# Start of a two-block transformer forward on one core: the transpose of the first norm weights as a step of its own, warm-up transposes 14 + 24 made 16 + 18, and new step orders

## What is computed

```python
# first block: layer 0 (differential attention), layer 1 (causal attention)
z = rmsnorm(x, a_norm_attn) @ a_w_in                      # q, k, v, memory queries
kv = rmsnorm(mem, a_mem_norm) @ a_w_mem_kv                # memory keys and values
x = x + concat(diff_attention(q, k, v), memory_attention(qm, mem)) @ a_w_out
x = x + square(relu(rmsnorm(x) @ a_w_up)) @ a_w_down      # hidden 4096
...                                                       # layer 1: kv, b_w_in, memory, MLP
x = rmsnorm(x, final_norm)
# second block
qa, c, iq, ik, iw, qb, kb, vb, gb = split(rmsnorm(x) @ w_in_2)
out_a = indexed_sparse_attention(qa, c, iq, ik, iw, rel_bias_2)   # top 64 keys
out_b = silu(gb) * group_norm(retention(qb, kb, vb))
x = x + concat(out_a, out_b) @ w_out_2
x = x + (silu(h @ w_gate_2) * (h @ w_up_2)) @ w_down_2    # hidden 2816
```

## Time and profile before

| | |
|---|---|
| median of 3 runs | 928.08 us (926.46 to 929.03) |
| the profiled execution | 928.42 us |
| its span, first to last instruction | 926.7 us |
| outside the span | 1.7 us |
| PE busy | 917.0 us (99%) |
| DVE busy | 574.1 us (62%) |
| ACT busy | 473.4 us (51%) |

### The profile page before, as it was taken

One profiled execution on the slowest core, in us unless ns is written; L12 is line 12 of the kernel. 1 busy time (PEld: TensorE's weight loads), 2 busy tenths in 40 slices (PEclk: granted clock), 3 DMA queues, 4 the chain that ended last, 5 costly groups with the idle time before them and its releaser, 6 DMA issues.

```text
span 926.7 us, 13209 instructions
## 1 busy us (share of the span) xinstructions
PE 917.0 (99%) x4740; PEld 768.6 (83%) x4740; DVE 574.1 (62%) x779; ACT 473.4 (51%) x718; POOL 55.2 (6%) x126
## 2 busy tenths in 40 slices
PE   8999999999999999999999999999999999999998
PEld 7778788888888888788888888888887888888886
DVE  4768658655555668365855655677886555444453
ACT  5866557444444566654644444556456463444441
POOL 1202121000000000000200000002130010000000
PEclk9999999999999999999999999999999999999999
DMA  8945135655556534234755555455613255556541
GB/s 290 334 137 165 65 137 196 222 196 201 184 182 191 171 137 136 92 113 147 262 188 198 199 186 183 152 174 179 197 63 128 92 181 182 181 183 197 189 155 46
DMA packets 95435, 157.77 MB, mean 170 GB/s; under 512 B 5928, under 2 KB 37624, under 8 KB 95392
## 3 DMA queue, kind: packets, MB, share of 16 engines
q1 hardware_dynamic: 93824, 155.08, 50.1%
q10 hardware_dynamic: 1536, 2.11, 0.7%
q0 software_dynamic: 32, 0.02, 0.0%
HBM read 156.12 MB, written 1.06 MB: 170 GB/s over the span
## 4 chain that ended last, share of the span: by engine, by line
PE 96%; DVE 2%; issue 1%; ACT 1%; DMA 0%; ACTq 0%; POOL 0%
PE proj L1563 10%; PE proj L1565 10%; PE proj L1564 10%; PE score L1563 6%; PE score L1564 6%; PE score L1565 6%; PE outp L1565 6%; PE outp L1563 6%; PE outp L1564 6%; PE turn L1622 6%; PE proj L1622 6%; PE turn L1626 3%; PE proj L1626 3%; PE turn L1609 2%; PE outp L1812 2%; PE score L1774 2%
## 5 line engine op out<-in xcount | busy, mean ns | idle before, releaser
L1904 DVE TENSOR_TENSOR wlo<-raw,whi 128x2048 fp32r<-128x2048 f32 (+1 forms) x131 | 297.7, 2277 | 192.5 <-ACT whi L1331 147.6
L1331 ACT ACTIVATE whi<-raw 128x2048 fp32r<-128x2048 f32 x64 | 122.6, 1916 | 170.0 <-PE outp L1565 57.5
L1563 PE MATMUL proj<-whi,set 128*128 128x512 f32 (+1 forms) x428 | 169.5, 396 | 1.0 <-DVE set L2069 1.0
L1565 PE MATMUL proj<-whi,set 128*128 128x512 f32 (+1 forms) x428 | 165.7, 387 | 0.0
L1564 PE MATMUL proj<-wlo,set 128*128 128x512 f32 (+1 forms) x428 | 165.2, 386 | 0.0
L1320 ACT ACTIVATE whi<-raw 128x2048 fp32r<-128x2048 f32 (+1 forms) x67 | 126.7, 1897 | 51.4 <-PE outp L1565 17.2
L1563 PEld LDWEIGHTS proj<-whi,set 128*128 128x128 f32 x428 | 80.4, 188 | 17.9 <-issue 1.7
L1565 PEld LDWEIGHTS proj<-whi,set 128*128 128x128 f32 x428 | 80.3, 188 | 16.8
L1564 PEld LDWEIGHTS proj<-wlo,set 128*128 128x128 f32 x428 | 80.5, 188 | 14.9
L1563 PE MATMUL score<-whi,set 128*128 128x512 f32 x236 | 92.9, 393 | 0.0
L1563 PE MATMUL outp<-whi,set 128*128 128x512 f32 x236 | 92.4, 391 | 0.0
(11 more groups left out here) (228 smaller groups left out, 1171.9 us busy)
## 6 DMA issues: line engine op xcount, KB each, us to landing
raw<-in_a_w_up SPq DMA_DIRECT2D x32, 512.0 KB, 4.2
raw<-in_a_w_down SPq DMA_DIRECT2D x32, 512.0 KB, 4.2
raw<-in_b_w_up SPq DMA_DIRECT2D x32, 512.0 KB, 4.2
raw<-in_b_w_down SPq DMA_DIRECT2D x32, 512.0 KB, 4.6
raw<-in_w_gate SPq DMA_DIRECT2D x22, 512.0 KB, 4.0
raw<-in_w_up SPq DMA_DIRECT2D x22, 512.0 KB, 5.0
raw<-in_w_down SPq DMA_DIRECT2D x22, 512.0 KB, 4.1
raw<-in_a_w_in SPq DMA_DIRECT2D x20, 512.0 KB, 7.1
```

The source lines that it names most:

```text
L1331: act.activation(shaped(whi, u), shaped(raw, u), ACT.Copy).then_inc(hi_done, 1)
L1563: pe.matmul(out_, hi, wh, start=start, stop=False)
L1565: return pe.matmul(out_, lo, wh, start=False, stop=stop)
L1904: return dve.tensor_tensor(shaped(wlo, u)[:, ks, :], shaped(raw, u)[:, ks, :], shaped(whi, u)[:, ks, :], ALU.subtract)
```

## The change

1. A new step `first_gains` stands in the list behind `turn_operand 0` and `1`. PE's part of it is `turn_gains(0)` and then `warm_up(WARM[1])`; DVE's part is the copy to `gcol`. `setup` keeps PE's wait and `warm_up(WARM[0])`.
2. `WARM` is (16, 18) where it was (14, 24). The warm-up behind `turn_operand 1` is gone.
3. `MOVES` is new for all three engines. Its last pair for PE is `("first_gains 0", "turn_operand 0")`, and its last two for DVE are `("turn_operand 1", "turn_operand 0")` and `("first_gains 0", "turn_operand 1")`. Run through the list, they give PE: `setup`, `first_gains`, `turn_operand 0`, `turn_operand 1`, `multiply 0`; and DVE: `first_gains`, `turn_operand 1`, `turn_operand 0`, `split 0`. ACT's first eight steps are as before, save that `square_sum 0` now stands ahead of `turn_operand 4`.
4. DVE waits for `ka_done` ahead of `retention_out 0`.

```diff
@@ MOVES, "PE" (last entries)
-        ("multiply 9", "turn_heads 3"), ("turn_operand 7", "multiply 3"), ("turn_operand 6", "turn_operand 7"),
-        ("multiply 2", "turn_operand 6"),
+        ("turn_operand 7", "multiply 3"), ("turn_operand 6", "turn_operand 7"), ("multiply 2", "turn_operand 6"),
+        ("first_gains 0", "turn_operand 0"),
@@ MOVES, "DVE" (last entries)
-        ("turn_operand 7", "split 4"), ("turn_operand 6", "split 3"), ("split 2", "turn_operand 6"),
+        ("turn_operand 6", "split 4"), ("turn_operand 7", "turn_operand 6"), ("split 2", "split 3"),
+        ("turn_operand 1", "turn_operand 0"), ("first_gains 0", "turn_operand 1"),
...
-WARM = (14, 24)
+WARM = (16, 18)
@@ the list of steps
         m1 = [turn_mem(0)]
+        add("first_gains")
         split(1)
@@ PE
                 if st.kind == "setup":
                     pe.wait_ge(consts_made, 1)
                     warm_up(WARM[0])
+                elif st.kind == "first_gains":
                     turn_gains(0)
+                    warm_up(WARM[1])
...
                     turn_bank(n, lambda t, k: st.src[:, t, k * P:(k + 1) * P], [k0, k0 + 1])
-                    if st.name == "turn_operand 1":
-                        warm_up(WARM[1])
@@ DVE
-                if st.kind == "setup":
+                if st.kind == "first_gains":
                     dve.wait_ge(s_full, 1)
...
                 elif st.kind == "retention_out":
                     dve.wait_ge(o_full, st.o + 1)
+                    if st.p == 0:
+                        dve.wait_ge(ka_done, NT)
```

## The result

The changed kernel takes 932.23 us in the median of four runs (932.10 to 934.07), the kernel before 928.08 (926.46 to 929.03): 4.15 us more, ratio 1.0059 (1.0046 to 1.0072). The profiled execution is the slowest of the four, 934.07 us with a span of 932.3. The forecast was 928.7 with a range to 932.2 and slower at 0.24.

A forecast was written before the change was run, and what follows sets the result against it. PE was taken to bound the kernel, busy 917.0 of 926.7 us. The start's +1.4 and the later orders' -0.8 gave +0.6 on the median of 928.08: 928.7 us, with a range of 926.0 to 932.2.

The forecast's parts named there:

- The order at the start: PE's start: norm weights still first, 18 warm-ups ahead of the mem transposes, `multiply 0` at 13.7 for 12.35, +1.4 us.
- the term for the granted clock behind the gap: First products behind PE's new 2 us gap from 11.7: no cost for a low clock in the sum.
- rival A: PE's gap at the start: level rises late or falls, first products run at 1.2 GHz; +3.7, 931.8 us; chance 0.17.
- The prediction's own sign of being wrong: First products at the start: matmuls of 0.43 us following PE's gap would show the forecast wrong.
- the -0.8 for the orders: Later orders: PE's 1.0 and 0.7 us waits around the group norm could go; half taken, -0.8 us.
- DVE's wait for `ka_done`: Ahead of `retention_out 0`: waits for DVE's own step some 15 steps earlier, holds nothing behind it; cost 0.
- the two more warm-ups at first: First warm-up on PE, 16 for 14: ends at 5.3, covered by the wait for the norm weights; cost 0.
- DVE's bank 1 ahead of bank 0: Operand copies at the start: DVE starts only when ACT has done both banks at 12.35, ending at 13.65.
- Rival C: First warm-ups: 16 lift PE's clock before 6.4, `multiply 0` at 11.6; -1.5, 926.5 us; chance 0.10.
- Rival D: PE's start: mem transposed ahead of the norm weights as the title says, `multiply 0` at 10.7; 925.6 us; chance 0.05.

The follow-up runs named there:

- the start alone: Kernel before with only the changed start (first_gains and 18 warm-ups ahead of the mem transposes, 16 first, DVE bank 1 first), all other orders as before: 931.61 us.
- the orders alone: Kernel before with the changed kernel's later orders and its wait for `ka_done`, keeping its own start (14 and 24 warm-ups): 928.83 us.
- the twelve: Kernel before with 12 warm-ups behind the mem transposes in place of 24: 926.87 us.
- the table load behind: Changed kernel with one ACT pair left out, so turn_weights 33 stands ahead of exps 34 again: 930.22 us.
- Memory first: Kernel before with the changed start, but PE transposes mem first, then the norm weights, then 18 warm-ups, DVE's order to suit: 925.62 us.
- gap filled: Changed kernel with 18 more warm-ups behind turn_operand 1, in PE's gap ahead of the first multiply: 930.38 us.
- memory first with the new orders: Changed kernel with only its first entries mended (PE takes mem, then first_gains; DVE first_gains, bank 0, bank 1), later orders kept: 929.00 us.
- memory first with twelve: Kernel before with mem transposed ahead of the norm weights and 12 warm-ups behind these in place of 18 (`WARM = (16, 12)`): 925.55 us.
- no warm-ups: Kernel before with no warm-ups behind the mem transposes in place of 24 (`WARM = (14, 0)`): 928.68 us.

## Why the forecast was wrong

**The order at the start** was read rightly. PE still waited for the norm weights, the 18 warm-ups stood between them and `mem`, and the first product came at 13.79 where the forecast had 13.7. The gap was 2.1 us for 2. In the changed kernel's own profile that closeness is partly luck: the transposes began at 10.01, not 10.8, since the first of the 18 ran at the full level, and took 1.70 us, not 0.88, since the level had fallen. In the start alone the terms themselves came out: the 18 end at 10.67 and the first product starts at 13.85.

**The step that failed at the start is the term for the granted clock behind the gap, which the likeliest sum put at nothing.** The forecast left 0.17 to rival A, a level that is low behind that gap. It came in five runs of six (the start alone), and its price was 1.9 (931.6 for 929.72), for 2.1 in rival A. The argument against it was that no row showed a fall. But no row of before showed PE resting for 2 us soon after a rise either, so that was no evidence. The prediction's own sign of being wrong, matmuls of 0.43 us behind the gap, came. The rule of the Trainium skill, "TensorE: Matmul & The Clock Gate", Part 1, was weighed as something for single runs. The traces agree that the level comes down around rests and that the moment differs from run to run: the 18 warm-ups ahead of `mem` take 2.11 to 4.03 us in the profiles of the changed start. For the chance it was read too weakly.

Rival A's 931.8 lies near the measured 932.23, but its sum isn't what happened either. It had 4.5 us for the start, where 3.7 came, and -0.8 for the orders, which cost time.

**The step that failed behind it is the -0.8 for the orders.** Its sign was wrong. The forecast followed DVE's queue and PE's, and both came out: the waits of 1.0 and 0.7 around the group norm went. It didn't follow ACT's, where `exps 34` now stood between two copies of weights, with a table load of 1.28 us in front. The waits rose by 0.8 (3.9 for 3.1), measured as +0.74 in the stretch. On top came one fall at 704.5 in the profiled run, 1.7 us. With the start of before, the orders cost 2.2 to 2.4 in every group of runs (the orders alone); that the medians differ by 0.9 only is a matter of which groups the runs came from.

**Together,** the two losses don't simply add up to the 4.15 of the whole. Two of the four runs, 932.10 and 932.22, have by their clock (0.998) one fall. The 931.6 of the start alone and the 0.74 of the orders' waits make 932.3, so a fall at the start and none in the stretch would give such a run; no profile of one was taken. The run that was profiled, 934.07, has three.

**No cost, as forecast:** DVE's wait for `ka_done` and the two more warm-ups at first show no wait in the trace. DVE's bank 1 ahead of bank 0 wasn't tried alone; by the chain it was worth some 0.1 us at most, since the first half of `whi` was ready just before the first product began. Rival C's early rise was real, and not only with 16: with 14 the profiles of the orders alone and of the twelve have it too. It is likely what makes the fastest group of before, of which no run was profiled. With the changed start it came with a fall behind it in the one profile that has it whole (the table load behind, 929.97).

**Rival D** was worked out to 925.6 with the gain around the group norm of 0.8. Memory first gave 925.62 with the orders of before, so without that gain. The sum was right by luck, through two errors: the first product came 1.1 earlier than worked out, and there was no 0.8.

What stays open: why in a given run the level falls in one gap and not in another. With the same 1.7 us wait, by the clocks, the changed kernel's orders gave no fall (gap filled, six of seven runs), always one (orders alone), or none to three (memory first with the new orders). The place of the wait in the run differed by some us between these, and that was not varied on purpose.

## What to carry to other kernels

Fillers that keep TensorE's clock up belong where the engine waits for work made from its own last output, not ahead of that output. Behind the transposes 24 of them gave 928.1 and 12 gave 926.9, ahead of them 18 gave 931.6. (The 925.6 of memory first has a second cause: `mem` no longer waits for the norm weights.) A gap of 2 us at the start cost itself and, in five runs of six, as much again for the fall behind it, so read the granted clock of each run beside its time, and the spacing of the matmuls beside both. When an order is changed, follow every engine's queue to where a function of another table set comes in, for a load of 1.28 us in the wrong place is longer than most of the waits that a planner trades in. When few runs are at hand, sort them into groups before comparing medians: the new orders cost 2.4 us in each group and 0.9 in the median. And compare a planner's output with its intention: here one pair of names undid it.

## What the runs showed of the hardware

- The level can be up already when the first 14 or 16 warm-ups are through: in three profiles (orders alone and twelve with 14, memory first with twelve with 16) the eight `mem` transposes, begun between 5.4 and 6.7 us, take 1.0 to 1.1 us, in the others that have them at this place 1.7 to 1.9. In the orders alone the second `mem` transposes start 2.1 us earlier by it (14.42 for 16.49). It is the likely reason for the distance of 1.8 us between the groups of before at 926.3 and 928.1; what makes the one at 929.3 is open.
- A fall can come within a rest or after PE is at work again. The gap from 11.7 to 13.8 was over when the level fell at 15.0 (changed kernel), the one to 703.0 when it fell at 704.5, and the one to 13.85 when it fell at 14.2 (start alone). But the level fell at 11.5 in a gap that ended at 11.71 (table load behind), and at 696.2 in one that ended at 696.84 (memory first with the new orders). Each lasted some 3.4 us, the last 6.6.
- A profile doesn't show as low what lies ahead of its first change of level: in the earlier trace rows the column reads 1.00 while eight transposes take 1.9 us, and in "no warm-ups" while products take 0.43 us each. Their spacing has to be read.
